# Gate/up and q/k products with high and low input in one 512-column matmul

## The reference, cut to what matters

```python
# first block
x = x + 0.5 * swiglu_ffn(rmsnorm(x), w_gate, w_up, w_down)     # 1024 -> 2816 -> 1024
x = x + hybrid_mixer(rmsnorm(x), ...)                          # 8 heads of 64, and a pooled half
x = x + 0.5 * swiglu_ffn(rmsnorm(x), w_gate, w_up, w_down)     # other weights
x = rmsnorm(x, final_norm)
# second block, two layers: x = layer_norm(2**0.5 * x + mixer(x))
#   "fox": q, k, v, f_logit, gate = x @ w_in; attention with a cumulative log-sigmoid bias
#   "dsa": index scores, top 64 keys per token, latent keys and values expanded by w_uk, w_uv
def swiglu_ffn(x, w_gate, w_up, w_down):
    return (silu(x @ w_gate) * (x @ w_up)) @ w_down
```

## Time and profile before

| | |
|---|---|
| median of 3 runs | 738.09 us |
| the profiled execution | 737.6 us |
| its span (first to last recorded instruction) | 735.8 us |
| mean granted clock of PE | 0.993 of full speed |
| PE busy | 718.9 us (98%) |
| DVE busy | 441.7 us (60%) |
| ACT busy | 353.4 us (48%) |
| POOL busy | 64.6 us (9%) |
| HBM traffic | 174 GB/s over the span |

### The profile page before, as it was taken

The page is one execution under the profiler, slowest core; times in us unless marked ns, Lnnn a source line. Parts: engine busy times, 40 slices in busy tenths (PEclk is TensorE's granted clock), DMA queues, the critical chain, the costliest instruction groups (busy, mean ns, idle before and its releaser), DMA issues.

```text
span 735.8 us, 11350 instructions
## 1 busy us (share of the span) xinstructions
PE 718.9 (98%) x4596; PEld 647.3 (88%) x4596; DVE 441.7 (60%) x709; ACT 353.4 (48%) x462; POOL 64.6 (9%) x36
## 2 busy tenths in 40 slices
PE   7899999999999999999999999999999999998995
PEld 7899999988888788999999988889998888876884
DVE  4675565655467436755665655575552637795756
ACT  6644433453475545644333443476334524576451
POOL 0000000000000420000000000000006342140002
PEclk9999999999999999999999999999999999999998
DMA  8986544555436324655544556435554314543001
GB/s 278 364 315 244 193 175 171 178 201 192 172 130 268 118 102 185 229 183 197 191 172 171 180 210 241 172 143 202 197 192 178 143 58 125 179 155 114 1 1 57
DMA packets 20678, 128.36 MB, mean 174 GB/s; under 512 B 2432, under 2 KB 3328, under 8 KB 6432
## 3 DMA queue, kind: packets, MB, share of 16 engines
q1 hardware_dynamic: 20304, 127.54, 47.9%
q10 hardware_dynamic: 288, 0.16, 0.1%
q0 software_dynamic: 48, 0.13, 0.0%
HBM read 126.77 MB, written 1.05 MB: 174 GB/s over the span
## 4 chain that ended last, share of the span: by engine, by line
PE 95%; ACT 1%; DVE 1%; DMA 1%; issue 1%; SPq 0%
PE ps L366 29%; PE ps L368 29%; PE ps L367 29%; PE ps L557 1%; DMA raw<-in_gu 1%; PE ps L900 1%; PE ps L377 1%; PE ps L613 1%; PE ps L614 1%; PE ps L612 1%; PE ps L728 1%; ACT whi L972 1%; PE ps L432 0%; PE ps L882 0%; PE ps L603 0%
## 5 line engine op out<-in xcount | busy, mean ns | idle before, releaser
L366 PE MATMUL ps<-xth,whi 128*128 128x256 f32 x832 | 237.6, 286 | 5.4 <-DVE wlo L1496 2.9
L367 PE MATMUL ps<-xtl,whi 128*128 128x256 f32 x832 | 236.7, 285 | 0.0
L368 PE MATMUL ps<-xth,wlo 128*128 128x256 f32 x832 | 236.6, 284 | 0.0
L1360 DVE TENSOR_TENSOR wlo<-raw,whi 128x2048 fp32r<-128x2048 f32 x68 | 156.8, 2314 | 68.1 <-ACT whi L972 68.0
L972 ACT ACTIVATE whi<-raw 128x2048 fp32r<-128x2048 f32 x78 | 148.7, 1909 | 92.2 <-PE ps L368 89.6
L366 PEld LDWEIGHTS ps<-xth,whi 128*128 128x128 f32 x832 | 161.1, 194 | 6.2 <-DVE wlo L1360 2.7
L367 PEld LDWEIGHTS ps<-xtl,whi 128*128 128x128 f32 x832 | 161.2, 194 | 0.1
L368 PEld LDWEIGHTS ps<-xth,wlo 128*128 128x128 f32 x832 | 161.0, 193 | 0.0
L366 PE MATMUL ps<-whi,xth 128*128 128x512 f32 (+1 forms) x304 | 121.5, 400 | 0.8 <-ACT work L1265 0.7
L368 PE MATMUL ps<-whi,xtl 128*128 128x512 f32 (+1 forms) x304 | 117.1, 385 | 0.0
L367 PE MATMUL ps<-wlo,xth 128*128 128x512 f32 (+1 forms) x304 | 116.8, 384 | 0.0
(11 more groups left out here) (202 smaller groups left out, 667.1 us busy)
## 6 DMA issues: line engine op xcount, KB each, us to landing
raw<-in_gu SPq DMA_DIRECT2D x41, 1024.0 KB, 4.8
raw<-in_dn SPq DMA_DIRECT2D x22, 1024.0 KB, 4.7
raw<-in_win SPq DMA_DIRECT2D x8, 1024.0 KB, 4.8
raw<-in_fqk SPq DMA_DIRECT2D x8, 1024.0 KB, 4.9
raw<-in_wout SPq DMA_DIRECT2D x4, 1024.0 KB, 4.8
raw<-in_fg SPq DMA_DIRECT2D x4, 1024.0 KB, 4.8
raw<-in_fv SPq DMA_DIRECT2D x4, 1024.0 KB, 4.8
raw<-in_fo SPq DMA_DIRECT2D x4, 1024.0 KB, 4.8
```

The costliest lines, as they stand in the source:

```text
L366: pe.matmul(o, xh, wh, start=start, stop=False)
L367: pe.matmul(o, xh, wl, start=False, stop=False)
L368: return pe.matmul(o, xl, wh, start=False, stop=stop)
L1360: dve.tensor_tensor(wlo[:, c % RING, 0:n], raw[:, c % RING, 0:n], whi[:, c % RING, 0:n].bitcast(F32), ALU.subtract).then_inc(lo_ready, 1)
```

## The change

**One 512-column matmul.** `xth` and `xtl` become the two halves of one tensor `xt` (for each k 256 high columns, then 256 low ones). `both_halves` replaces `three` in gate/up and q/k: `whi` times all 512 columns in one matmul (the high product left in the bank, the mixed one right), and `wlo` times `xth` in one of 256 columns, added to the right half. Gate and up (or q and k) now take a bank each, so four chunks in flight take all 8 banks. Reading out takes more: ACT copies the right halves of both banks to SBUF (`cross`), DVE adds the left halves (`sum_halves`, frees the banks), and multiplies by the row (`times_row`, SBUF only), 512 columns each. The row's bank is 7, and PE waits for the row's copy before chunk 3 writes there. `rstd_to_row` now stands between chunks 2 and 3 in the first FFN (the second: between 1 and 2, as before). q/k has two pairs of banks in turn instead of four banks.

**First loads.** The second chunk's first piece is issued by SP, and both chunks' second pieces by ACT.

**Key and value copies.** Two of four key copies and two of four value copies go to DVE; gate and turned queries use other banks.

**Last normalisation.** ACT scales and shifts in one pass, the left half of tile 0 alone; POOL has two operations instead of four, and DVE takes the right half of tile 0.

```diff
-        xth = sb("xth", [P, KD, S], F32R)
-        xtl = sb("xtl", [P, KD, S], F32R)
+        xt = sb("xt", [P, KD, 2, S], F32R)
+        xth, xtl = xt[:, :, 0, :], xt[:, :, 1, :]
...
-                for c in range(2 if i else 1):
+                for c in range(0 if i == 1 else 2):
...
-            for n in range(2 * NT):
+            for n in (1, 0, 2, 3):
                 t, half = n // 2, slice(n % 2 * BANK, (n % 2 + 1) * BANK)
-                sp.wait_ge(y_by_dve if t else y_by_pool, n % 2 + 1)
+                if n:
+                    sp.wait_ge(y_by_dve, n)
+                else:
+                    sp.wait_ge(y_by_pool, 1)
                 sp.dma_start(out[t * P:(t + 1) * P, half], X[:, t, half]).then_inc(y_stored, 16)
...
+            def both_halves(bank, wh, wl, k, first, last):
+
+                x = xt[:, k, :, :].rearrange("p a s -> p (a s)")
+                small = ps[:, bank, S:2 * S], wl, xth[:, k, :]
+                if last:
+                    pe.matmul(*small, start=False, stop=False)
+                    return pe.matmul(ps[:, bank, :], wh, x, start=False, stop=True)
+                pe.matmul(ps[:, bank, :], wh, x, start=first, stop=False)
+                return pe.matmul(*small, start=False, stop=False)
 
...
-                    for n_step, (k, u) in enumerate(steps):
-                        if f == 0 and static and j == 0 and i == 3 and n_step == KD:
-                            rstd_to_row(0, DOWN, ffn_diag)
-                        if f == 1 and static and j == 0 and i == 0:
+                        steps = [(k, u) for u in range(2) for k in range(KD)]
+                    for k, u in steps:
+                        if static and j == 0 and i == 3 and u == 1 and k == 0:
...
-                        m = three(ps[:, banks[u], u * S:(u + 1) * S], wh[:, w], wl[:, w], xth[:, k, :], xtl[:, k, :], k == 0, k == KD - 1)
+                        m = both_halves(2 * i + u, wh[:, w], wl[:, w], k, k == 0, k == KD - 1)
...
-                    if f == 1 and i == 1:
-                        rstd_to_row(1, DOWN, ffn_diag)
+                    if i == 2 - f:
+                        rstd_to_row(f, ROW, ffn_diag)
...
+                pe.wait_ge(gu_read, NG * f + 20)
...
-                if h == 0:
+                if h == 1:
                     pe.wait_ge(f_order, 1)
-                if h == 1:
                     pe.wait_ge(row_ready, 3)
-                if h >= 4:
-                    pe.wait_ge(qk2_ready, 2 * (h - 3))
+                if h >= 2:
+                    pe.wait_ge(qk2_ready, 3 * (h - 2) + 1)
                 for n in range(2):
...
-                        m = three(ps[:, 4 + h % 4, n * S:(n + 1) * S], wh[:, w], wl[:, w], xth[:, k, :], xtl[:, k, :], k == 0, k == KD - 1)
+                        m = both_halves(4 + 2 * (h % 2) + n, wh[:, w], wl[:, w], k, k == 0, k == KD - 1)
...
+                def cross(j, i):
+                    act.wait_ge(chunk_used, C_GU[f] + i + 1 + 4 * j)
+                    if not (isinstance(j, int) and f + j == 0 and i < 2):
+                        act.wait_ge(h_done, NG * f + i - 1 + 4 * j)
+                    act.activation(gu_sb[:, i % 2, :, :], ps[:, 2 * i:2 * i + 2, S:2 * S], ACT.Copy).then_inc(cross_copied, 1)
...
+                    cross(0, 0)
+                    cross(0, 1)
                     norm(0)
                     hi(C_GU[f] + RING)
+                    row(f, ROW, ffn_row)
                     load_table(ACT.Silu)
-                    row(f, DOWN, ffn_row)
                     hi(C_GU[f] + 1 + RING)
...
-            act.dma_start(raw[:, 1, 0:S], a["gu0"][1][:, 0:S]).then_inc(part_landed[1], 16)
+            for c in range(2):
+                act.dma_start(raw[:, c, S:2 * S], a["gu0"][c][:, S:2 * S]).then_inc(part_landed[2 + c], 16)
...
-            for p in range(4):
+            for p in range(2, 4):
...
-                for t in range(NT):
-                    act.wait_ge(v_psum, 2 * nb + t + 1)
-                    act.activation(v3[:, t, nb * BANK:(nb + 1) * BANK], ps[:, 2 + t, :], ACT.Copy).then_inc(v3_ready, 1)
+                act.wait_ge(v_psum, 2 * nb + 1)
+                act.activation(v3[:, 0, nb * BANK:(nb + 1) * BANK], ps[:, 2, :], ACT.Copy).then_inc(v_act, 1)
...
-            for h in range(2):
-                x = X[:, 0, h * BANK:(h + 1) * BANK]
-                act.wait_ge(last_stats, 1)
-                act.activation(x, x, ACT.Identity, bias=neg_mean).then_inc(last_centred, 1)
-                act.wait_ge(last_stats, 2)
-                act.wait_ge(last_centred, h + 1)
-                act.activation(x, x, ACT.Copy, scale=rstd[:, 0:1]).then_inc(last_normed, 1)
+            act.wait_ge(last_stats, 2)
+            act.activation(X[:, 0, 0:BANK], X[:, 0, 0:BANK], ACT.Identity, bias=neg_mean, scale=rstd[:, 0:1]).then_inc(last_normed, 1)
...
-                def gate_and_up(j, i):
-
-                    dve.wait_ge(chunk_used, C_GU[f] + i + 1 + 4 * j)
-                    if not (isinstance(j, int) and f + j == 0 and i < 2):
-                        dve.wait_ge(h_done, NG * f + i - 1 + 4 * j)
-                    dve.tensor_tensor(sg_sb[:, i % 2, :], ps[:, GU + i, 0:S], ffn_row, ALU.mult).then_inc(gate_scaled, 1)
-                    up_bank = GU + i
-                    if isinstance(j, int) and j == 0:
-                        up_bank = [DOWN + 1, DOWN + 2, DOWN + 3, 3][i] if f == 0 else [3, 1, 2, 3][i]
-                    dve.tensor_tensor(up_sb[:, i % 2, :], ps[:, up_bank, S:2 * S], ffn_row, ALU.mult).then_inc(gu_read, 1)
+                def sum_halves(j, i):
+
+                    dve.wait_ge(cross_copied, NG * f + i + 1 + 4 * j)
+                    g = gu_sb[:, i % 2, :, :]
+                    dve.tensor_tensor(g, ps[:, 2 * i:2 * i + 2, 0:S], g, ALU.add).then_inc(gu_read, 1)
+
+                def times_row(j, i):
+
+                    dve.wait_ge(gu_read, NG * f + i + 1 + 4 * j)
+                    g = gu_sb[:, i % 2, :, :]
+                    dve.tensor_tensor(g, g, ffn_row.unsqueeze(1).broadcast_to([P, 2, S]), ALU.mult).then_inc(gate_scaled, 1)
 
...
+                sum_halves(0, 0)
                 if f == 0:
+                    sum_halves(0, 1)
                     norm(0)
                     dve.wait_ge(eye_landed, 16)
                     diagonal(0, ffn_diag)
                 lo(C_GU[f] + RING)
+                if f:
+                    sum_halves(0, 1)
+                dve.wait_ge(row_ready, f + 1)
+                times_row(0, 0)
+                times_row(0, 1)
+                hidden(0, 1, 0)
                 lo(C_GU[f] + 1 + RING)
-                dve.wait_ge(row_ready, f + 1)
-                for i in range(4):
-                    gate_and_up(0, i)
-                    if i:
-                        hidden(i - 1, i, i - 1 & 1)
-                    if i >= 2:
-                        lo(C_GU[f] + i + RING)
+                for i in range(2, 4):
+                    sum_halves(0, i)
+                    times_row(0, i)
+                    hidden(i - 1, i, i - 1 & 1)
+                    lo(C_GU[f] + i + RING)
...
+                dve.wait_ge(chunk_used, C_FQK + h + 1)
+                bank = 4 + 2 * (h % 2)
+                dve.wait_ge(cross_copied, 2 * NG + h + 1)
+                dve.tensor_tensor(qk_sum[:, h % 2, :, :], ps[:, bank:bank + 2, 0:S], qk_sum[:, h % 2, :, :], ALU.add).then_inc(qk2_ready, 1)
+                dve.wait_ge(qk2_ready, 3 * h + 1)
+                dve.scalar_tensor_tensor(out=q2t[:, h, :], in0=qk_sum[:, h % 2, 0, :], scalar=SCALE2, in1=rstd_row, op0=ALU.mult, op1=ALU.mult).then_inc(qk2_ready, 1)
+                dve.tensor_tensor(k2t[:, h, :], qk_sum[:, h % 2, 1, :], rstd_row, ALU.mult).then_inc(qk2_ready, 1)
...
+            for p in range(2):
+                dve.wait_ge(k_psum, p + 1)
+                dve.tensor_copy(k3t[0:NOPE, 2 * p:2 * p + 2, :].rearrange("p h s -> p (h s)"), ps[0:NOPE, p, :]).then_inc(k3_ready, 1)
...
+                if h == 1:
+                    for nb in range(2):
+                        dve.wait_ge(v_psum, 2 * nb + 2)
+                        dve.tensor_copy(v3[:, 1, nb * BANK:(nb + 1) * BANK], ps[:, 3, :]).then_inc(v_dve, 1)
```

More of the change, by code:

```diff
@@ L1160, in _ @@
                     act.activation(ncum_hi, ncum, ACT.Copy).then_inc(cum_hi, 1)
+                act.wait_ge(chunk_used, C_FQK + h + 1)
+                if h >= 2:
+                    act.wait_ge(qk2_ready, 3 * (h - 1))
+                bank = 4 + 2 * (h % 2)
+                act.activation(qk_sum[:, h % 2, :, :], ps[:, bank:bank + 2, S:2 * S], ACT.Copy).then_inc(cross_copied, 1)
                 hi(C_FQK + h + RING)
@@ new lines, in _ @@
+            centre(X[:, 0, right], right, 0)
+            dve.wait_ge(ln_order, 10)
+            finish(X[:, 0, right], right, 0)
+            for nb, c in enumerate((left, right)):
+                dve.wait_ge(chunk_used, C_DO + 3 + nb)
+                i = last_residual(1, c, bns[:, 1, nb, :])
+            i.then_inc(ln_order, 1)
```

(11 more changed lines are left out.)

153 lines of the change are left out of this document (92 added, 61 removed).

## The result

The changed kernel takes 725.27 us (median; 725.21 to 725.71) beside 738.31 us (737.51 to 739.55) of the kernel before on the same chip: ratio 0.9823, 95% interval 0.9806 to 0.984. The forecast was 722.8 us with a range of 720.0 to 727.5. The sign and the range held; the gain was 13.0 us where 15.3 was forecast. In the profiled executions 737.6 us became 725.27, and the span 723.5, which is 12.3 us less. It is this 12.3 that has to be accounted for.

A forecast was written before the change was run, and what follows sets the result against it. PE, busy 98% of the span, was taken as the bound; matmuls 10.3, opening 4.2, keys and values 0.3 and end 0.5 gave 15.3 us, so 738.1 became 722.8 us. The range was 720.0 to 727.5 us, at 80%.

The forecast's parts named there:

- The matmuls: Gate/up and q/k: one 512-column matmul replacing two of 256 saves 13.4 ns per piece, 10.3 us over 48 chunks.
- Rival (a): Gate/up and q/k: the fixed part stays through weight loads, a pair takes 360 ns, kernel 734.0 us; chance 8%.
- The estimate of 2.1 us: Gate/up and q/k: saving from 832 removed matmuls by the Trainium skill's 2.5 ns gap, in place of 11.1 us.
- The other engines: Each chunk: DVE is done 4.8 us after a chunk's end, within 5.55 us, so the added work costs nothing.
- Rival (c): Gate/up and q/k: reading out the banks becomes the bound and the kernel gets slower, 749 us; chance 3%.
- The opening: First FFN: banks freed before the row remove the wait at chunk 4 and the slow stretch; 4.2 us gained.
- (b): First FFN: the row is late, PE waits 2 us or more before chunk 3 and runs slow; 725.3 us, 14%.
- (d): First FFN: banks are freed early but the wait at chunk 4 stays, for late low parts; 726.1 us, 5%.
- First loads: Start: third pieces come one issue, 0.45 us, earlier, but the row's chain decides; taken as 0.
- they do not bind: Transfers: need 4% more per us; 266 GB/s in one opening window against a mean of 174, so no limit.
- Keys and values: Key and value copies: two of each four on DVE shorten PE's wait; 0.3 us, bounds 0 and 0.6.
- The end: Last normalisation: fewer POOL operations save 0.8 us, a drawn-out DVE operation may cost 0.7; 0.5 taken, bounds 0.2 and 0.9.

The follow-up runs named there:

- split kernel: The changed kernel with each 512-column matmul split again into two of 256 columns: 731.83 us, 6.2 above the unaltered changed kernel.
- grouped kernel: The changed kernel with seven 512-column matmuls, eight of 256, then the last of 512 per half chunk (gate/up outside the opening, q/k): 723.23 us.
- late banks: The changed kernel with DVE's sums for chunks 0 and 1 of the first FFN put back behind the low parts of chunks 4 and 5: 727.12 us.
- end-as-before kernel: The changed kernel with the last normalisation and the order of its stores as in the kernel before: 726.57 us.

## Why the prediction was right and where it was wrong

- **The matmuls: the step that failed in size.** The forecast had 13.4 ns per pair and 0.214 us per chunk, 10.3 us over 48 chunks. Measured were 0.12 us per chunk, 5.9 us (2.2 + 2.7 + 1.0 above), and 6.2 us for all 52 by the split kernel. The argument was that two widths with the same fixed part of 13.4 ns keep it when they stand beside each other. Each fixed part was read from a run of one width. In the mixed order the pair pays some 6 ns more, because the order changes width at every step. The working bounded this by 0 and 11.1 and took the upper end; the truth lay in the middle. It also said that the trace has no 256-column matmul right behind one of 512, and that is wrong. The trace of the kernel before has both changes of width, where a gate/up stage ends (its last 256-column matmul starts at 140.99 us) and where one begins:

```profile
141.11 0.40 PE L366 MATMUL ps<-whi,hth 128*128 128x512 f32 x1
...
142.27 0.39 PE L368 MATMUL ps<-whi,htl 128*128 128x512 f32 x1
```

```profile
288.34 0.39 PE L368 MATMUL ps<-whi,xtl 128*128 128x512 f32 x1
288.57 0.28 PE L366 MATMUL ps<-xth,whi 128*128 128x256 f32 x1
288.68 0.28 PE L367 MATMUL ps<-xtl,whi 128*128 128x256 f32 x1
```

From 141.11 to 142.27 us there are five steps of 512 columns: 1.16 us, where five times 226.6 ns are 1.13. To the nanosecond they are 233, 236, 228, 232 and 232, the sequence of the grouped kernel, and the first step of 256 columns at 288.57 is 113. The first gaps alone add up to 346 ns, so these rows don't give the 352.5 of strict alternation; but they show that the steady gaps don't hold at a change of width, and that made the full 13.4 ns doubtful. Rival (a) had the right place and too high a price; its mechanism, the weight loads, was not tested. The estimate of 2.1 us from the formula of the Trainium skill ("TensorE: Matmul & The Clock Gate", section "Back-to-back issue gap") was a third of the measured 6.2: the removed fixed part is larger than the page's, even after what the mixture takes.
- **The other engines: right.** DVE done 4.9 us behind a chunk's end (4.8 forecast), no wait of PE in the loop, prices of 597 and 690 ns. Rival (c) did not come up.
- **The opening: right in mechanism, 1.0 us too small.** No wait at chunk 4, clock 1.00, gain 5.2 (4.2 forecast). The late banks brought a wait back. Rivals (b) and (d) did not come up. The missing 1.0 is the next point. The 1.21 us of wait before the row's matmuls (0.9 forecast) is near by luck: PE was at the end of chunk 2 at 24.86 us and not at 26.3, as there was no first stretch of slow clock, and the diagonals came 1.2 us earlier too. That a wait of 1.21 us left the clock at 1.00 was read from a window six us later; the windows from 673 to 680 us have 1.00 too.
- **First loads: wrong.** They were set at nothing because "the row's chain decides". But that chain begins with the landing of chunk 3, as the same paragraph said, and so it moves with it: 1.1 us earlier in the profiled execution, 0.6 in the medians. The step asked only what the third pieces gain, not what each later transfer in the same queue gains: SP issued chunk 3 at 9.55 us in place of 10.90. And "they do not bind" was read from the window of 36 to 40 us; from 12 to 20 us, where chunk 3 is on its way, the DMA engines of before are busy throughout (0.99 and 1.02).
- **Keys and values: right.** 0.3 of 0.3. The wait for keys fell from 1.21 to 0.73 us, and the one behind the value copies grew from 0.69 to 0.83 and gave some back, as the working said.
- **The end: upper bound.** 0.9 in the profile for 0.5 forecast, 0.6 by the medians. No operation of DVE was drawn out beside POOL. The rule of the Trainium skill that spoke for the lower bound ("SBUF — State Buffer", section "SBUF: two separate sides") fits what came: in the end-as-before kernel POOL's operation began first, at 718.15 us, and DVE's at 718.73 took 1.56 us; in the kernel after DVE's L1912 began first, at 714.07, and POOL's from 714.39 took 1.57. What failed is the step from the rule to the lower bound: the working did not ask which of the two begins first.

By the profile the sum is 5.9 + 5.2 + 0.3 + 0.9 = 12.3 us for 15.3 forecast: the matmuls 4.4 too high, the opening with the loads 1.0 and the end 0.4 too low. The median, 725.3, lies outside the forecast's own bounds (720.5 to 724.5). The range went on to 727.5 for the cases (b) and (d), and neither happened; that it holds the median is in part luck. Errors of both signs cancelled in part as well: with the matmuls' error of 4.4 us alone the time would have been 727.2.

## What to carry to other kernels

Read the price of a matmul from neighbours like those that it will have: a rate measured in a run of one width doesn't hold for a sequence of mixed widths. If widths must mix, collect them: here one change of width per chunk in place of one per pair gave 3.8 us for nothing but another order. Look for such neighbours at the borders between stages too. When an issue is taken off a queue, move everything behind it in that queue, and follow the chain that begins with the last of these transfers. And look at the mean granted clock of each run of the kernel before: a gain over an execution with slow stretches is not the gain over one without.

## What the runs showed that was not expected

A change of width between neighbouring matmuls has a price of its own. Behind a run of 256 columns (120 ns apart) the first 512-column matmuls start 233, 236, 228, 233 and 230 ns apart before they settle at 226 to 227; behind a run of 512 the first gap of 256 columns is 113 to 114 ns, once, and then 119 to 120. In strict alternation the pair stays at 352.5 ns; grouped by eight it is 349, by sixteen 348, and 346.6 would be the sum of the two steady gaps. The sequence of gaps is the same in every chunk, and in the kernel before at the border of a stage (141.11 us above), whatever ACT and DVE do beside it, which speaks against contention. Which part of the engine causes it, no run here tells.
